# Attention scores of a hybrid encoder layer: low keys stacked by head, and output weights split in the projection

## What is computed

```
h    = rmsnorm(x, g_norm_mix)
proj = h @ w_in            # queries, keys, values of 8 near heads; 8 window heads with 2 key heads
# near: each query sees a window of 8 x 16 grid neighbours, with a learned bias
logits = einsum('bnmqhd,bnmkhd->bnmhqk', qb, kb) * scale + bias ; masked ; softmax ; @ v
# window: |q - k| <= 128, 4 query heads on each key head, with a sink logit in the softmax
o = concatenate([rmsnorm(oa, g_out_na), rmsnorm(ob, g_out_swa)])
x = x + o @ w_out
x = x + (silu(rmsnorm(x) @ w_gate) * (rmsnorm(x) @ w_up)) @ w_down ; then a last rmsnorm
```

## Time and profile before

| | us |
|---|---|
| median of 3 runs | 2259.54 |
| lowest, highest | 2259.07, 2263.42 |
| the profiled execution | 2259.97 |
| its span, first to last instruction | 2258.2 |
| PE busy in it | 2208.8 (98%) |
| DVE busy | 1440.5 (64%) |
| ScalarE busy | 922.3 (41%) |
| GpSimd busy | 327.8 (15%) |

### The profile page before, as it was taken

How to read it: one execution, slowest core, us unless ns; L and a number is a source line. 1 busy time by engine, 2 the same in 40 slices (tenths; PEclk the granted TensorE clock), 3 DMA queues, 4 the chain that set the end, 5 groups by cost and what they waited for, 6 DMA issues and landing times.

```text
span 2258.2 us, 33189 instructions
## 1 busy us (share of the span) xinstructions
PE 2208.8 (98%) x11464; PEld 1818.5 (81%) x11464; DVE 1440.5 (64%) x2747; ACT 922.3 (41%) x1824; POOL 327.8 (15%) x304
## 2 busy tenths in 40 slices
PE   7999999999999999999999999999999999999998
PEld 6888888788877788778888887888888877888886
DVE  4412143399899777776666657665656578565776
ACT  4411121288888633343333334433333333131342
POOL 3370001145334100011212120000000002020100
PEclk9999999999999999999999999999999999999999
DMA  6472425789954275675545457323232286353544
GB/s 225 140 186 99 140 87 148 201 217 246 235 143 111 83 226 200 224 265 175 189 165 199 154 209 263 128 80 131 80 131 73 102 305 234 104 177 108 191 145 152
DMA packets 274677, 376.68 MB, mean 167 GB/s; under 512 B 15258, under 2 KB 182306, under 8 KB 269168
## 3 DMA queue, kind: packets, MB, share of 16 engines
q1 hardware_dynamic: 266528, 354.15, 49.3%
q0 software_dynamic: 5568, 11.87, 2.0%
q10 hardware_dynamic: 2448, 8.91, 1.4%
HBM read 237.77 MB, written 140.31 MB: 167 GB/s over the span
## 4 chain that ended last, share of the span: by engine, by line
PE 89%; DVE 6%; DMA 2%; issue 2%; ACT 1%; POOL 0%; DVEq 0%; ACTq 0%; SPq 0%
PE late_psum L2047 11%; PE late_psum L2048 11%; PE late_psum L2049 11%; PE late_psum L2078 6%; PE late_psum L2080 5%; PE late_psum L2079 5%; PE late_psum L1017 4%; PE late_psum L997 4%; PE late_psum L527 3%; PE late_psum L528 3%; PE late_psum L529 3%; PE late_psum L555 3%; PE late_psum L554 3%; PE late_psum L556 3%; PE late_psum L985 2%; PE late_psum L1396 2%
## 5 line engine op out<-in xcount | busy, mean ns | idle before, releaser
L2047 PE MATMUL late_psum<-ff_h,ff_ring 128*128 128x512 f32 x1232 | 479.9, 390 | 5.9 <-DVE ff_acts L1907 3.0
L2049 PE MATMUL late_psum<-ff_h,ff_ring 128*128 128x512 f32 x1232 | 479.3, 389 | 0.0
L2048 PE MATMUL late_psum<-ff_h,ff_ring 128*128 128x512 f32 x1232 | 479.3, 389 | 0.0
L2047 PEld LDWEIGHTS late_psum<-ff_h,ff_ring 128*128 128x128 f32 x1232 | 231.2, 188 | 55.9 <-DVE ff_h L1868 3.9
L2049 PEld LDWEIGHTS late_psum<-ff_h,ff_ring 128*128 128x128 f32 x1232 | 231.2, 188 | 48.1
L2048 PEld LDWEIGHTS late_psum<-ff_h,ff_ring 128*128 128x128 f32 x1232 | 231.2, 188 | 47.7
L2078 PE MATMUL late_psum<-ff_d,ff_a 128*128 128x512 f32 x616 | 240.6, 391 | 8.3 <-DVE ff_x L1967 5.3
L2079 PE MATMUL late_psum<-ff_d,ff_a 128*128 128x512 f32 x616 | 239.7, 389 | 0.0
L2080 PE MATMUL late_psum<-ff_d,ff_a 128*128 128x512 f32 x616 | 239.7, 389 | 0.0
L1967 DVE TENSOR_TENSOR ff_x<-late_psum,ff_x 128x512 f32<-128x512 f32 x224 | 153.6, 689 | 121.4 <-PE late_psum L2080 121.0
L1863 DVE TENSOR_TENSOR ff_ring<-ff_raw,ff_ring 128x512 fp32r<-128x512 f32 x176 | 127.5, 726 | 104.3 <-ACT ff_ring L1740 104.1
(11 more groups left out here) (159 smaller groups left out, 4148.9 us busy)
## 6 DMA issues: line engine op xcount, KB each, us to landing
acts_scratch<-ff_acts SPq DMA_DIRECT2D x22, 1792.0 KB, 7.8
ff_a<-acts_scratch SPq DMA_DIRECT2D x24, 960.0 KB, 5.1
ff_raw<-in_w_gate SPq DMA_DIRECT2D x44, 512.0 KB, 3.8
ff_raw<-in_w_up SPq DMA_DIRECT2D x44, 512.0 KB, 3.9
ff_d<-down_scratch SPq DMA_DIRECT2D x21, 768.0 KB, 6.3
att_q_stack<-qk_scratch SPq DMA_DIRECT2D x56, 256.0 KB, 5.2
ffn_in_scratch<-mix_h_stage SPq DMA_DIRECT2D x8, 1792.0 KB, 6.2
ff_h<-ffn_in_scratch SPq DMA_DIRECT2D x14, 1024.0 KB, 7.6
```

The source lines that it names most:

```text
L2047: pe.matmul(out_bank, whi[:, k], hhi[:, :, k], start=(k == 0 and not onto), stop=False, skip_group_check=onto)
L2048: pe.matmul(out_bank, whi[:, k], hlo[:, :, k], start=False, stop=False, skip_group_check=onto)
L2049: last = pe.matmul(out_bank, wlo[:, k], hhi[:, :, k], start=False, stop=(k == 3), skip_group_check=onto)
```

## The change

Three things are changed.

The high keys stay stacked twice (`k_hi`). The low keys of both heads are kept once, head 0 in rows 0 to 63 and head 1 in rows 64 to 127 (`k_lo`). The queries of head 1 are stacked the other way round (low above high), so that each head's high queries stand in the same rows as its low keys. A low matmul multiplies only the high queries with the low keys, in 64 rows; the product of low queries and low keys is no longer computed.

`score` does both heads of a tile at every even step and nothing at odd steps: high of head 0, high of head 1, low of head 0, low of head 1. Loading queries takes four transfers instead of two for a quarter, loading keys three instead of four.

The output weights are multiplied by the gains and split during the first 16 query and key steps, by ScalarE (high) and DVE (low), and stored to a scratch tensor. GpSimd in attention only loads them into `w_pool`, eight transfers of 1 MB.

```diff
@@ project_phase
+    def load_out_weights(k):
+        if k == 0:
+            sp.wait_ge(turned, NT)
+        else:
+            sp.wait_ge(out_lo_done, k)
+        if k < 4:
+            sp.dma_start(out_raw[:], w_out[k * P:(k + 1) * P, :]).then_inc(out_in, 32)
+            return
+        for e in range(2):
+            r0 = AW + (k - 4 + 4 * e) * HD
+            sp.dma_start(out_raw[e * HD:(e + 1) * HD, :], w_out[r0:r0 + HD, :]).then_inc(out_in, 16)
+    def store_out_weights(k):
+        sp.wait_ge(out_lo_done, k + 1)
+        sp.dma_start(out_dram[k], out_parts[:].bitcast(F32)).then_inc(out_stored, 16)
+    def out_weights_hi(k):
...
+        act.wait_ge(out_in, 32 * (k + 1))
+        if k >= 1:
+            act.wait_ge(out_stored, 16 * k)
+        nc.scalar.mul(out_parts[:, 0], out_raw[:], gains[:, k:k + 1]).then_inc(out_hi_done, 1)
+    def out_weights_lo(k):
+        dve.wait_ge(out_hi_done, k + 1)
+        nc.vector.scalar_tensor_tensor(out=out_parts[:, 1], in0=out_raw[:], scalar=gains[:, k:k + 1],
+                                       in1=out_parts[:, 0], op0=ALU.mult, op1=ALU.subtract).then_inc(out_lo_done, 1)
@@ sync, behind the stores of step j
+            if j < 2 * KT:
+                (store_out_weights if j % 2 else load_out_weights)(j // 2)
             if j == 3:
                 for n in range(8, 12):
                     load_w(n)
@@ scalar, behind the high part of step j (vector likewise with out_weights_lo)
+            if j < 2 * KT and j % 2:
+                out_weights_hi(j // 2)
@@ gpsimd, ahead of the value stores
+            pool.dma_start(gains[:, 0:4], g_na.rearrange("a (k p) -> p (a k)", p=P)).then_inc(gains_in, 16)
...
@@ attention_phase
+    def half_of(part, e):
+        row = (part + e) % 2 * HD
+        return slice(row, row + HD)
     def load_q(kind, r, b):
...
+        for part in range(2):
+            for e in range(2):
+                head = bass.ds(2 * r + e, 1) if kind.near else bass.ds(2 * NAH - NEAR_ROUNDS + r + SWH // SWKV * e, 1)
+                sp.dma_start(f32(q_st[half_of(part, e), e:e + 1, qs]), heads[part, :, head, qs]).then_inc(q_in[b], 16)
     def load_k(kind, r, b):
...
+        for twice in range(2):
+            sp.dma_start(f32(k_hi[twice * HD:(twice + 1) * HD, :, ks]), heads[0, :, pair, ks]).then_inc(k_in[b], 16)
+        sp.dma_start(f32(k_lo[:, ks]), qk_dram[1, both, ks]).then_inc(k_in[b], 16)
@@ gpsimd in attention
+        proj.out_weights_stored(pool)
         for k in range(KT):
...
+            pool.wait_ge(shifted, UNITS * (NEAR_ROUNDS + 1) + 12 * k)
+            if k == 0:
+                pool.wait_ge(pv_done, NEAR_PT_BUFS // 2 + NT * NEAR_ROUNDS)
+            pool.dma_start(f32(w_pool[:, k::KT, :]), out_dram[k]).then_inc(out_weights_in, 16)
@@ score
-        e, t = u % 2, u // 2
...
+        if u % 2:
+            return
+        t = u // 2
...
-        pe.wait_ge(shifted, UNITS * (r + 1) - SC_BUFS + u + 1)
-        q, out = q_st[:, e, t * P:(t + 1) * P], sc[:, u % SC_BUFS, 0:n]
-        pe.matmul(out, q, kind.keys(k_st[:, e, 0, :], t), start=True, stop=False)
-        pe.matmul(out, q, kind.keys(k_st[:, e, 1, :], t), start=False, stop=True).then_inc(scored, 1)
+        pe.wait_ge(shifted, UNITS * (r + 1) - SC_BUFS + u + 2)
+        q, out = [q_st[:, e, t * P:(t + 1) * P] for e in range(2)], [sc[:, (u + e) % SC_BUFS, 0:n] for e in range(2)]
+        for e in range(2):
+            pe.matmul(out[e], q[e], kind.keys(k_hi[:, e, :], t), start=True, stop=False)
+        for e in range(2):
+            rows = half_of(0, e)
+            pe.matmul(out[e], q[e][rows], kind.keys(k_lo[rows], t), start=False, stop=True).then_inc(scored, 1)
```

More of the change, by code:

```diff
@@ L301, in gpsimd @@
                 .then_inc(w_lo_by_pool, 1)
+        with nc.allow_non_contiguous_dma(reason="gains, one for each partition"):
+            pool.dma_start(gains[:, 0:4], g_na.rearrange("a (k p) -> p (a k)", p=P)).then_inc(gains_in, 16)
+            for e in range(2):
+                pool.dma_start(gains[e * HD:(e + 1) * HD, 4:8],
+                               g_swa[:, e * 4 * HD:(e + 1) * 4 * HD].rearrange("a (k p) -> p (a k)", p=HD)) \
+                    .then_inc(gains_in, 16)
         for t in range(NT):
@@ L475, in vector @@
             low.then_inc(res_lo, 1)
+            if j < 2 * KT and j % 2:
+                out_weights_lo(j // 2)
             for n in split_at(V_STEPS + j):
@@ L655, in attention_phase @@
     bias_made, sinks_negated = sem("bias_made"), sem("sinks_negated")
-    w_in, gains_in = [sem(f"w_out_in{i}") for i in range(2)], sem("gains_in")
-    w_scaled, w_hi_done, w_lo_done = sem("w_scaled"), sem("w_hi_done"), sem("w_lo_done")
+    out_weights_in = sem("out_weights_in")
     scored, shifted, exped = sem("scored"), sem("shifted"), sem("exped")
@@ L734, in load_k @@
         pair = bass.ds(NAH + 2 * r, 2) if kind.near else slice(2 * NAH + SWH, HEADS)
[L735 to L738, removed]
+        both = bass.ds((NAH + 2 * r) * HD, P) if kind.near else slice((2 * NAH + SWH) * HD, HEADS * HD)
+        for twice in range(2):
+            sp.dma_start(f32(k_hi[twice * HD:(twice + 1) * HD, :, ks]), heads[0, :, pair, ks]).then_inc(k_in[b], 16)
+        sp.dma_start(f32(k_lo[:, ks]), qk_dram[1, both, ks]).then_inc(k_in[b], 16)
     def load_v(kind, r, b):
@@ L771, in load_first_q @@
     def load_first_q(part):
-        pair = slice(0, 2)
-        sp.dma_start(f32(q_st[part * HD:(part + 1) * HD, :, :]), heads[part, :, pair, :]).then_inc(q_in[0], 16)
+        for e in range(2):
+            sp.dma_start(f32(q_st[half_of(part, e), e, :]), heads[part, :, e, :]).then_inc(q_in[0], 16)
         if part == 1:
             for b in range(1, 4):
-                sp.sem_inc(q_in[b], 32)
+                sp.sem_inc(q_in[b], 64)
     def load_first_k(piece):
[L781 to L786, removed]
+        if piece < 2:
+            sp.dma_start(f32(k_hi[piece * HD:(piece + 1) * HD, :, :]), heads[0, :, NAH:NAH + 2, :]).then_inc(k_in[0], 16)
+            return
+        sp.dma_start(f32(k_lo[:]), qk_dram[1, NAH * HD:(NAH + 2) * HD, :]).then_inc(k_in[0], 16)
+        for b in range(1, 4):
+            sp.sem_inc(k_in[b], 48)
     def load_first_v(b):
@@ L848, in gpsimd @@
             make_bias(r)
[L851 to L862, removed]
-        for k in range(KT):
-            raw, w_hi, w_lo = w_raw[:, k % 2, :], w_pool[:, k, :], w_pool[:, KT + k, :]
-            pool.wait_ge(w_in[k % 2], 32 * (k // 2 + 1))
-            wait_units(3 * k)
-            nc.gpsimd.tensor_scalar(raw, raw, gcol[:, k:k + 1], None, ALU.mult).then_inc(w_scaled, 1)
-            pool.wait_ge(w_scaled, k + 1)
-            wait_units(3 * k + 1)
-            nc.gpsimd.tensor_copy(w_hi, raw).then_inc(w_hi_done, 1)
-            pool.wait_ge(w_hi_done, k + 1)
-            wait_units(3 * k + 2)
-            nc.gpsimd.tensor_tensor(w_lo, raw, w_hi, ALU.subtract).then_inc(w_lo_done, 1)
-            if k + 2 < KT:
-                pool.wait_ge(w_lo_done, k + 1)
-                load_w(k + 2)
+        proj.out_weights_stored(pool)
+        for k in range(KT):
+            pool.wait_ge(shifted, UNITS * (NEAR_ROUNDS + 1) + 12 * k)
+            if k == 0:
+                pool.wait_ge(pv_done, NEAR_PT_BUFS // 2 + NT * NEAR_ROUNDS)
+            pool.dma_start(f32(w_pool[:, k::KT, :]), out_dram[k]).then_inc(out_weights_in, 16)
     def exp(kind, r, u):
```

63 lines of the change are left out of this document (33 added, 30 removed).

## The result

| | before | after |
|---|---|---|
| median, us | 2260.26 (6 runs) | 2276.03 (6 runs) |
| lowest, highest | 2259.07, 2263.42 | 2269.42, 2277.02 |
| the profiled execution | 2259.97 | 2276.91 |
| its span | 2258.2 | 2274.8 |

What follows compares the result with a forecast made beforehand. PE's own work was taken to bound attention's rounds. 2259.5 + 26.7 (scores: low matmuls saved, switches added) - 5.6 (waits returned) = 2280.6, other terms 0, said as 2280; its own range 2268 to 2290, the whole range 2234 to 2300.

Steps and rivals of the forecast that it cites:

- PE's own work bounds both: Attention's near and window rounds: PE's work fills 40.6 of 42.0 us and 36.5 of 37.5, the rest waiting.
- (a): Scores: low matmuls in different row halves run side by side, saving one of two, 0.18, 0.24 or 0.12 us a tile.
- third rival: Scores: the halves don't overlap fully, weight loads or matmuls follow each other; 2294 to 2304, said 2298; chance 0.14.
- (b): Scores: two more array switches per tile, into split rows and back, taken at 2 x 0.20 = 0.40 us.
- sign that would have spoken against the forecast: Scores in attention: the forecast is wrong if low weights load while the high matmuls still run; no size given.
- first rival: Scores: rows split without a switch, DVE taking over near rounds at some 39.5 us; 2237; chance 0.24.
- the second (2254): Scores: emptying but hidden weights, two switches at 0.09 us, with the waits returned 2254; chance 0.12.
- the pair order: Attention: the pair waits for a bank half a step earlier, but no wait ends later; 0 to +2 us.
- 44.4 and 40.3: Attention: forecast lengths in us of near rounds (44.4) and window rounds (40.3).
- the waits returned: Attention: GpSimd's passes go, DVE gets lighter and waits shrink, 3.2 us window, 2.4 near; -5.6 us (0 to -9.6).
- the projection: Query and key projection: added weight multiplies, subtracts, loads and stores are hidden; cost 0, at worst +3 us.
- The clock rival: Start of attention: emptying gaps might lower PE's clock to 1.2 GHz; called small, left in the range, no own chance.

Runs made afterwards that it cites:

- e10: Kernel before plus both heads of a tile scored in one step with 128-row matmuls, and output weights split in the projection, loaded a step early: 2249.43 us (0.9952).
- e8: Changed kernel with both low matmuls of a tile in the same (upper) half of the array's rows: 2300.9 us, one run.
- e6: Changed kernel with each output weights load issued right behind the store of the block before, one step earlier: 2267.57 us (1.0037).
- e9: Changed kernel with all 128 low score matmuls left out: 2237.42 us, one run.
- e5: Kernel before with both heads of a tile scored in one step, order high, high, low, low, all matmuls with 128 rows: 2253.88 us (0.9971).
- e11: Kernel before with both heads scored in one step, 128 rows, order high, low of head 0, then high, low of head 1: 2252.49 us (0.9962).
- e1: Kernel before with only the stacked low keys and the new score: 2266.15 us (1.0029).
- e2: Kernel before with only the output weights prepared in the projection: 2263.73 us (1.0011).
- e3: Changed kernel with the four input weights loads of step 3 issued one each at steps 3, 5, 7 and 9: 2275.13 us (1.0062).
- e4: Changed kernel with transposes ahead of the scores in each step of PE: 2271.9 us (1.0043).
- e7: Kernel before with output weights split in the projection, each load issued one step earlier, scores as before: 2257.92 us (0.9988).

## Why the prediction was right, and where it was not

2280 was forecast and 2276 measured, but that the two are so close is luck: the sum came out by terms that offset each other. Attention was forecast at +21.1 and gave +6.0; the projection and the end were forecast at 0 and gave +7.1 and +4.1 in the profiled execution.

**Right: what bounds it.** "PE's own work bounds both", and the prices of the score matmuls, transposes, pairs and value runs held. With the value run's new exit in the pair order (about 0.05 us cheaper, see below) they give 40.2 us for a near round without waits and 35.7 for a window round; e10 measured 40.39 and 35.75.

**Right: halves side by side (a).** 3 to 4 ns apart in after, and e8 is what their following each other would have cost. The third rival, 2298, falls for after; the 24 us that it put on matmuls one behind the other are what e8 lost, 24.9.

**Right in kind, mis-sized: the switches (b).** Taken at 2 x 0.20 = 0.40 a tile, each an emptying of 0.09 and an exposed weight load of 0.11. The parts are there: 0.09 on the way in, 0.10 for the lows' load, 0.09 on the way back, 0.06 for the transposes' load, 0.34 in all. The transposes' load is the part that was too dear. By the tile of e10 it is 0.18 + 0.18 = 0.36 (what a tile measured and what a low matmul saves). The sign that would have spoken against the forecast, low weights loading while the high matmuls run, did not appear: the loader stood idle for 0.25 us before them. Starts in the tiles of 512 columns give 0.34 as well, so the term comes to 19 to 20 us over 128 tiles; +26.7 was forecast and 18.1 is what the medians of e6 and e10 give. The first rival (no switch, 2237) and the second (2254) both fall: their 384-column tile would be at -0.18 and 0.00, and it is at +0.18. The second had the emptying right and took the loads to be hidden. The first rival's floor was nearly right: DVE ended e9's near round at 38.64, where 39.5 was said, and its window round took 32.38 with DVE busy 31.94, where about 32 was said.

The Trainium skill, page TensorEngine Tiling (Array Packing), section Key Properties, says that a change of tiling mode drains TensorE. For row splits these traces now agree, with 0.09 us on entering (after) and 0.09 on leaving (e8). The Trainium skill, page TensorE: Matmul & The Clock Gate, section Why this matters for your kernels, says that small-K matmuls in distinct row groups run at the same time; starts 3 to 4 ns apart in after, and 0.17 us a tile lost in e8, agree.

**Wrong: the pair order, "0 to +2 us".** e5 gives -6.5 and e11 -8.1. The text looked only for a wait that ends later and did not ask which waits end earlier, nor what follows the value runs. It had priced the exposed weight load of the score behind a value run at 0.11 us itself; with transposes behind it instead, about 0.05 of each run's 0.34 comes back, 0.4 us a near round and 0.8 a window round, and the rest of the gain is PE's waits. In after the same gain is inside the +6.0. Taken in two steps, from before to e10 and from e10 to after, a near round is 42.02 - 1.63 + 2.01 = 42.40, and a window round 37.40 - 1.65 + 2.84 = 38.59 (the 1.65 has 0.5 of the passes' removal in it). 44.4 and 40.3 were said.

**Wrong in its cause: the waits returned, -5.6.** They were put down to GpSimd's passes gone. In after none of the saving needs them: e1 has the passes and the same 38.59, and e6 (weights prepared, no wait in the projection) is 1.4 us above e1, less than runs of one kernel differ by. The passes' worth shows only where PE still waits: 1.0 us a window round in e2, 0.5 in e5 against e10. The normalise fell to 0.417 us on average, as said, with nothing gained by it.

**Wrong: the projection, "cost 0, at worst +3".** Two steps failed. The first is what stands behind the multiply: the text named the next result's copy, DVE's low part and PE's bank ("still under 16.8"), and left out the splits of the input weights, which go through the same two engines; it is for one of those that PE waited 4.2 us. The second is that it treated one late load as one stall; the loads, multiplies and stores form a loop of 11.0 us in 11.2 us of steps, so lateness stays. ScalarE stood for 17.2 us once, at 154 to 172, and PE stood at 215. The half clock behind PE's wait is worth 2.6 of the 7.1. e6 gives 8.5 us back, at the start of attention (440.61 against 449.10) as in the median; the kernels in which PE has no such wait start attention between 440.61 and 442.15, so the loss is 7 to 8.5.

**The clock at the start of attention and at the end.** The clock rival was left in the range. The half clock at the start of attention lasts 10.2 us instead of 6.8, which is worth at most 1.7 us of the first round's 47.26 against 45.30. It lasts 10.2 us or more in every kernel with the row split or the new loads of queries and keys (e1, e3, e4, e6, e8, e9) and in e2 and e7, and 6.8 or less in e5, e10, e11 and before; what decides it was not tried. The part behind the output projection is the same code in all thirteen profiled executions and took from 1283.29 us (before, the lowest) to 1290.07 (e8), so after's +4.1 there is no effect of the change that could be shown. A stretch of 3.4 us at 1.2 GHz at 1929 us, which the kernel before has not, is at most 1.7 of it.

**Left open.** Why scoring a tile in one step removes PE's waits: that the two scores reach DVE together and its normalise is thereby earlier for the transposes is only argued. The queries' and keys' loads were not measured apart from the split; PE never waited for them.

## What to carry over

Price a split of the array by its way in and its way out against the matmul that it saves: here 0.34 to 0.36 us for two switches and the weight loads behind them, against 0.18. Before splitting, try the mere reordering that the split needs; here it was the part that paid. And a job added beside a busy pipeline is hidden only if its whole loop, transfer to transfer, is clearly shorter than its period (11.0 in 11.2 us was not), and if everything that queues behind it on its engines can wait that long: list all of it, not only the next result.

## What the runs showed of the hardware

Entering a row split cost 0.09 us in which PE empties (after) and leaving it 0.09 (e8), and neither way was the next weight load hidden: 0.10 us for the low halves, 0.06 in front of the transposes. By the same kind of reading the switch of columns showed 0.08, and 0.16 with a load of 0.05 in it. A stall of 4.2 us of PE in a stage that is otherwise full cost another 2.6 us by the clock at 1.2 GHz behind it. A normalise on DVE of 0.42 us takes up to 1.45 while GpSimd works on its passes, yet this cost only where PE had waits.
